# A decoder trunk on one core: two input projections of eight weight tiles turned from full products into seven products of quarters, with the sums of x made behind the memory weights

## The reference, cut to what matters

```python
proj = x @ w_in
cb, cc, ch, rq, rk, rv, rg, mq, gl = jnp.split(proj, split_idx, axis=-1)
conv_y, new_buf = short_conv(cc * ch, conv_buf, conv_w)
a_out = (cb * conv_y) @ w_conv_out
...                                            # retention branch: b_out
m_out = mem_attention(mq.reshape(b, t, MEM_HEADS, MEM_HEAD_DIM), mk, mv).reshape(b, t, MEM_WIDTH) @ w_mem_out
merged = g[:, :, 0] * a_out + g[:, :, 1] * b_out + g[:, :, 2] * m_out
x = layer_norm(DEEPNORM_ALPHA * x + merged @ w_out, ln1_g, ln1_b)
hdn = jnp.square(jax.nn.relu(x @ w_up))
x = layer_norm(DEEPNORM_ALPHA * x + hdn @ w_down, ln2_g, ln2_b)
```

## Time and profile before

| | |
|---|---|
| median of 3 runs | 2172.88 us (2172.08 to 2173.35) |
| the profiled execution, its own time | 2170.49 us |
| its span, first to last instruction | 2168.7 us |
| granted TensorE clock, mean | 0.993 |
| PE / PEld busy | 2127.2 us (98%) / 2081.6 us (96%), 16116 matmuls |
| POOL busy | 1326.5 us (61%) |
| DVE busy | 1081.6 us (50%) |
| ACT busy | 508.8 us (23%) |
| DMA | 215.23 MB, mean 99 GB/s |

### The profile page before, as it was taken

One profiled execution on the slowest core, in us unless ns is written; L12 is line 12 of the kernel. 1 busy time (PEld: TensorE's weight loads), 2 busy tenths in 40 slices (PEclk: granted clock), 3 DMA queues, 4 the chain that ended last, 5 costly groups with the idle time before them and its releaser, 6 DMA issues.

```text
span 2168.7 us, 39024 instructions
## 1 busy us (share of the span) xinstructions
PE 2127.2 (98%) x16116; PEld 2081.6 (96%) x16116; DVE 1081.6 (50%) x1713; ACT 508.8 (23%) x909; POOL 1326.5 (61%) x1545
## 2 busy tenths in 40 slices
PE   8999999999999999999999999999999999999997
PEld 8998999999998999999999989999999989999997
DVE  7156300543278873525791572006424787726257
ACT  3121111041013141414141210200410131514133
POOL 6644557645683948375866446676457759475574
PEclk9999999999999999999999999999999999999998
DMA  5314424234231323222324243342352313222321
GB/s 184 113 59 157 128 86 136 69 107 160 94 98 59 98 78 98 79 79 80 96 61 126 59 156 117 103 130 68 108 176 78 98 41 104 79 90 79 98 89 53
DMA packets 199928, 215.23 MB, mean 99 GB/s; under 512 B 5216, under 2 KB 192608, under 8 KB 199776
## 3 DMA queue, kind: packets, MB, share of 16 engines
q1 hardware_dynamic: 170304, 172.84, 25.6%
q10 hardware_dynamic: 29472, 40.20, 5.5%
HBM read 199.06 MB, written 13.97 MB: 98 GB/s over the span
## 4 chain that ended last, share of the span: by engine, by line
PE 94%; DVE 6%; issue 0%; ACT 0%; DMA 0%; ACTq 0%; DVEq 0%
PE gp L524 52%; PE gp L1038 12%; PE gp L540 7%; PE gp L550 7%; PE qb L630 6%; PE gp L693 4%; PE gp L867 1%; PE gp L879 1%; PE qb L661 1%; PE gp L688 1%; DVE r L2055 1%; DVE r L1946 1%; DVE dacc L1902 0%; DVE qb L1943 0%; DVE sqacc L1931 0%; DVE x_lo L1955 0%
## 5 line engine op out<-in xcount | busy, mean ns | idle before, releaser
L439 POOL TENSOR_TENSOR w_lo<-stage,w_hi 128x256 fp32r<-128x256 f32 x1072 | 869.2, 842 | 52.5 <-ACT w_hi L1250 30.0
L436 POOL TENSOR_SCALAR w_hi<-stage 128x1024 fp32r<-128x1024 f32 (+1 forms) x268 | 288.0, 1075 | 567.7 <-PE gp L524 256.9
L524 PE MATMUL gp<-x_hi,w_hi 128*128 128x288 f32 x1408 | 303.8, 297 | 0.0
L524 PE MATMUL gp<-b_hi,w_hi 128*128 128x288 f32 x1408 | 303.6, 297 | 0.0
L524 PE MATMUL gp<-x_lo,w_hi 128*128 128x288 f32 x1408 | 301.0, 295 | 0.0
L524 PE MATMUL gp<-x_hi,w_lo 128*128 128x288 f32 x1408 | 300.9, 295 | 0.0
L524 PE MATMUL gp<-b_lo,w_hi 128*128 128x288 f32 x1408 | 300.5, 295 | 0.0
L524 PE MATMUL gp<-b_hi,w_lo 128*128 128x288 f32 x1408 | 300.5, 295 | 0.0
L524 PEld LDWEIGHTS gp<-b_hi,w_hi 128*128 128x128 f32 x1408 | 226.5, 188 | 3.4 <-issue 3.1
L524 PEld LDWEIGHTS gp<-x_hi,w_hi 128*128 128x128 f32 x1408 | 226.8, 189 | 2.9 <-issue 2.6
L524 PEld LDWEIGHTS gp<-x_lo,w_hi 128*128 128x128 f32 x1408 | 226.6, 189 | 0.0
(11 more groups left out here) (275 smaller groups left out, 4368.0 us busy)
## 6 DMA issues: line engine op xcount, KB each, us to landing
stage<-in_w_in SPq DMA_DIRECT2D x62, 1024.0 KB, 5.8
stage<-in_w_up SPq DMA_DIRECT2D x32, 1024.0 KB, 5.4
stage<-in_w_down SPq DMA_DIRECT2D x32, 1024.0 KB, 5.0
stage<-in_w_ret_out SPq DMA_DIRECT2D x8, 1024.0 KB, 5.3
stage<-in_w_mem_kv SPq DMA_DIRECT2D x8, 1024.0 KB, 5.0
stage<-in_w_out SPq DMA_DIRECT2D x8, 1024.0 KB, 5.0
s_in_c<-in_ret_state ACTq DMA_DIRECT2D x8, 512.0 KB, 4.6
out_ret_sample<-s_in_c ACTq DMA_DIRECT2D x8, 512.0 KB, 3.4
```

The lines of the kernel that those rows point to most:

```text
L436: nc.gpsimd.tensor_scalar(hi, raw, 1.0, 1.0, ALU.mult, ALU.mult).then_inc(hi_done, 1)
L439: ins = nc.gpsimd.tensor_tensor(lo[:, k:k + 2, :], raw[:, k:k + 2, :], hi[:, k:k + 2, :].bitcast(F32), ALU.subtract)
L524: last = mm(gp[:, 2 * (i % 2) + half, 0:HALF], w[:, i % 4, k * P:(k + 1) * P], x(k, half), start=(n == 0), stop=(n == 3 * nk - 1))
```

## The change

`T_MQ` and `T_CC` are done as group 0 of seven products: four pairs, the first two giving `mq`, the last two `cc`. The sums of x for them lie in `q_hi` and `q_lo` (where `b_hi` and `b_lo` are, free there) and are made by DVE and ACT during `T_KV`; their scratch is `tmp`. The helpers take g, pair numbers count 16 a layer and not 12, and the functions move up in the file unchanged but for that. ACT's evacuation loop (L1273) goes. POOL makes for these tiles only the lows of the raw quarters. PE's wait for the sums of x stands inside `seven_products`, ahead of its third product, for group 0 and for group 1; before it stood ahead of group 1. `T_CH` and `T_CB` stay full products.

```diff
+    q_hi = place("q_hi", [P, 4, 4, HALF], F32R, a_bhi)
+    q_lo = place("q_lo", [P, 4, 4, HALF], F32R, a_blo)
     def pair_no(l, g, p):
+        return (l * 4 + g) * 4 + p
+    def hidden_no(l, g, p):
         return (l * 3 + g - 1) * 4 + p
+    def first_tile(g):
+        return T_FF + 16 * g if g else T_MQ
+    def out_of_pair(g, p):
+        return (relu, relu_odd)[p % 2] if g else (mq, cc)[p // 2][:, 2 * (p % 2):2 * (p % 2) + 2, :]
...
 POOL
-            with pool.Fori(0, (T_AM - T_MQ) // RING) as it:
-                split_four(l, it * RING + T_MQ)
+            seven_splits(l, 0)
+            split_four(l, T_CH, behind=(0, pair_no(l, 0, 3)))
+            split_four(l, T_CB)
...
 PE
-            with pe.Fori(0, 4) as j:
+            for p in range(4):
+                seven_products(0, p)
+            with pe.Fori(2, 4) as j:
                 for i in range(4):
                     product(l, j * 4 + T_MQ + i, j * 2 + (T_MQ + i) // 2, i, *X)
+                if p == 0 and g < 2:
+                    pe.wait_ge(s_split, l * 8 + 4 * g + 4)
                 pe.wait_ge(t_split, 4 * q + 1)
                 one(2, c, rows_sum(0), True)
...
-                    if g == 1:
-                        pe.wait_ge(s_split, l * 4 + 4)
...
 ACT
                 weights_high(T_KV + 4 + i)
+                if i % 2:
+                    sums_high(0, i // 2)
+            act.wait_ge(b_ready, l * 9 + 9)
             for i in (0, 2):
                 tile_is_done(act, l, T_KV + 5 + i)
...
+                if i == 0:
+                    raw_to_bank(0, 0)
+                    seven_high(0, 0, 0)
+                    seven_high(0, 0, 1)
+                    sums_high(0, 2)
+                else:
+                    seven_high(0, 0, 4)
+                    seven_high(0, 0, 2)
+                    sums_high(0, 3)
+                    seven_high(0, 0, 3)
+                    seven_high(0, 0, 5)
+                    seven_high(0, 0, 6)
             act.dma_start(kT_new[bass.ds(l, 1), :, :, :].rearrange("l p h m -> (l p) h m"), km[:, :, :]).then_inc(km_out, 16)
             act.dma_start(v_new[bass.ds(l, 1), :, :].rearrange("l (m p) c -> p (l m) c", p=P), vm[:, :, :]).then_inc(km_out, 16)
-            for t0, buf, s in ((T_MQ, mq, mq_ready), (T_CC, cc, cc_in)):
...
+            seven_aside(0)
...
 DVE, behind its last multiplication of T_RO
+            def x_total(g, k):
+                x_sum = x_sums if g else tmp
+                if k:
+                    dve.wait_ge(s_made, l * 8 + 4 * g + k)
+                for i in range(2):
+                    ins = vec_.tensor_tensor(x_sum[:, i, :], x_hi[:, 4 * i + k, :].bitcast(F32),
+                                             x_lo[:, 4 * i + k, :].bitcast(F32), ALU.add)
+                link(ins)
...
+            for k in range(4):
+                x_total(0, k)
+                if k:
+                    row_sums_low(0, k - 1)
+                x_parts(0, k)
+                if k == 2:
+                    weight_sum(0, 0, 1)
+            sum_low(0, 0, 1)
+            weight_sum(0, 0, 2)
+            weight_sum(0, 0, 3)
+            row_sums_low(0, 3)
+            sum_low(0, 0, 2)
+            weight_sum(0, 0, 4)
+            sum_low(0, 0, 3)
+            sum_low(0, 0, 4)
+            seven_aside(0, queries_or_gates)
```

More of the change, by code:

```diff
@@ new lines, in seven_high, with keep_part @@
+            def seven_high(g, p, n):
+                q = pair_no(l, g, p)
+                seven_free(act, l, g, p, n)
+                k_half, i = SEVEN[n]
+                if k_half is not None:
+                    act_fn(seven_slot(w_hi, n), quarter(p, k_half, i), ACT.Copy).then_inc(raw_high, 1)
+                else:
+                    act.wait_ge(t_made, 4 * q + i)
+                    act_fn(seven_slot(w_hi, n), t_sum((0, 1, 2, 3)[i - 1]), ACT.Copy).then_inc(t_high, 1)
+            def keep_part(q, n, bank, i):
+                act.wait_ge(prod_done, 7 * q + n + 1)
+                if q:
+                    act.wait_ge(quarter_made, 4 * (q - 1) + 4)
+                act_fn(part[:, i, :], gp[:, bank, 0:HALF], ACT.Copy).then_inc(part_in, 1)
@@ new lines, in hidden_high, with seven_aside @@
+            def hidden_high(g, p, i):
+                act.wait_ge(act_made, 2 * hidden_no(l, g, p) + 2 - i)
+                act_fn(b_hi[:, 2 * p + i, :], relu_of(p)[:, i, :], ACT.Copy).then_inc(act_high, 1)
+            def seven_aside(g):
+                for p in range(4):
+                    q, a, more = pair_no(l, g, p), (0, 3)[p % 2], p < 3
+                    if more:
+                        raw_to_bank(g, p + 1)
+                    keep_part(q, 0, a, 0)
+                    if more:
+                        seven_high(g, p + 1, 0)
+                    if g and p:
+                        hidden_high(g, p - 1, 0)
+                    if more:
+                        seven_high(g, p + 1, 1)
+                    keep_part(q, 2, 1, 1)
+                    if more:
+                        seven_high(g, p + 1, 2)
+                    keep_part(q, 3, a, 2)
+                    if more:
+                        seven_high(g, p + 1, 3)
+                        seven_high(g, p + 1, 4)
+                    keep_part(q, 5, a, 3)
+                    if more:
+                        seven_high(g, p + 1, 5)
+                    if g:
+                        hidden_high(g, p, 1)
+                    if more:
+                        seven_high(g, p + 1, 6)
@@ new lines, in seven_aside @@
+            def seven_aside(g, done):
+                for p in range(4):
+                    more = p < 3
+                    if more:
+                        weight_sum(g, p + 1, 1)
+                    quarter_out(g, p, 0)
+                    if more:
+                        sum_low(g, p + 1, 1)
+                        weight_sum(g, p + 1, 2)
+                        weight_sum(g, p + 1, 3)
+                        sum_low(g, p + 1, 2)
+                        weight_sum(g, p + 1, 4)
+                    quarter_out(g, p, 1)
+                    quarter_out(g, p, 2)
+                    done(p, 1)
+                    if more:
+                        sum_low(g, p + 1, 3)
+                    quarter_out(g, p, 3)
+                    done(p, 0)
+                    if more:
+                        sum_low(g, p + 1, 4)
```

314 lines of the change are left out of this document (129 added, 185 removed).

## The result

Over 15 runs of each the changed kernel takes 2181.95 us and the kernel before 2175.56. One of the 15 runs of the changed kernel took 7332 us and is left out of the ratio, the other 14 lie between 2176.5 and 2184.7: ratio 1.0028, interval 1.0019 to 1.0037. The forecast was 2176.6, 0.17% above a kernel before of 2172.88. The changed kernel is 5.4 us above the forecast, and 2.7 us of that is the kernel before itself, whose median is 2.7 us higher here and whose executions lie between 2171.6 and 2178.8. The profiled execution has a span of 2177.1 us where 2172.5 was forecast, at a mean granted clock of 0.988 (before 0.993).

A forecast was written before the change was run, and what follows sets the result against it. PE was taken to bound the kernel nearly throughout. Per layer -6.4 (fewer matmuls) - 2.2 (moved wait) + 6.0 (sums of x) + 4.5 (first pair) = +1.9, +3.8 in all: median 2176.6 us, range 2165.5 to 2182.

The forecast's parts named there:

- the first pair: First pair of products in T_MQ: PE waits at its third and fourth products, costing 4.5 us a layer, bounds 3 and 5.5.
- The third product: First pair in T_MQ: PE waits 2.5 us for DVE's last low of the sums of x.
- The fourth: First pair in T_MQ: the fourth product waits for ACT to copy the first one away, 2.0 us.
- Sums of x in the memory stage: Memory stage: DVE's sums slow POOL's lows, so PE waits at both value pairs; 6.0 us a layer, at most 10.5.
- rival 2: Memory stage: POOL and DVE take strict turns, costing 10.5 us a layer in place of 6.0; 2185.6 us, chance 0.07.
- Fewer matmuls: T_MQ and T_CC: 336 matmuls in place of 384 save 6.4 us a layer, 12.8 in all.
- Rival 4: T_MQ and T_CC: seven products not bound by PE, so 6.4 us a layer isn't saved; up to 2189 us, chance 0.04.
- The moved wait: Start of group 1: two products done first cover PE's wait for sums of x; gain 2.2 us a layer, 4.4 in all.
- Rival 3: Start of group 1: the moved wait gives nothing, as another input or `keep_part` is late; 2181 us, chance 0.05.
- Costed at nothing: Pairs 1 to 3, loading the first pair's weights, the end of pair 3 and ACT's removed copies: no time lost or gained.
- The sum: All terms: +1.9 us a layer, +3.8 in two layers; 2174.3 us profiled, 2176.6 as median, 0.17% above before.
- Rival 1: Memory stage: POOL's lows stay in time, so the 6.0 us loss drops out; 2164.7 us, chance 0.29.

The follow-up runs named there:

- e3: The changed kernel with idle matmuls filling PE's waits: 18 and 10 ahead of the two value pairs, 18 ahead of the third product. Ratio to the kernel before 1.0004.
- e6: The changed kernel with the totals of x for k = 0 to 2 partly in PSUM, so the parts read one SBUF input. Ratio to the kernel before 0.9988.
- e4: The changed kernel with group 0's sums of x made earlier, in T_RO, three of four totals in PSUM, two high parts moved ahead on ACT. 2154.0 us, ratio 0.9898.
- e5: The kernel before with one edit: PE's wait for group 1's sums of x stands ahead of its third product, not ahead of the group. Ratio 0.9965.
- e1: The kernel before with only the sums of x added in the memory stage on DVE and ACT, not used by anything. Ratio 1.0052.
- e2: The changed kernel without group 0's sums of x; products take quarters of x instead, so outputs differ. Ratio to the kernel before 0.9938.
- e7: The kernel before with three more POOL instructions ahead of the sixth memory tile's lows, no DVE work added. Memory stage through T_CC 82.35 / 82.33 us by layer, one execution.
- e8: The kernel before with five more POOL instructions ahead of the sixth memory tile's lows, no DVE work added. Memory stage through T_CC 85.19 / 83.69 us by layer, one execution.

## Why the prediction was right in direction and short in size

**The step that fell short is the price of a wait: the forecast put it at the length of the wait and put the granted clock behind it at nothing, without a reason.** The waits themselves it had right. Each is taken below from the starts of PE's matmuls. PE's timeline after, in layer 0, at the two waits of the first pair:

```profile
348.62 0.40 PE L917 MATMUL gp<-q_hi,w_hi 128*128 128x288 f32 x1 [2.52 <-DVE q_lo L1822]
...
352.24 0.58 PE L917 MATMUL gp<-q_hi,w_hi 128*128 128x288 f32 x1 [1.47 <-ACT part L1289]
...
354.05 0.44 PE L917 MATMUL gp<-q_lo,w_hi 128*128 128x288 f32 x1
354.29 0.44 PE L917 MATMUL gp<-q_hi,w_lo 128*128 128x288 f32 x1
...
357.16 0.29 PE L917 MATMUL gp<-q_hi,w_hi 128*128 128x288 f32 x1
357.29 0.30 PE L917 MATMUL gp<-q_lo,w_hi 128*128 128x288 f32 x1
```

At 354 the starts are 0.24 us apart, at 357 they are 0.13: TensorE's clock was at 1.2 GHz and then at 2.4 again. PE had been idle 2.5 us before 348.6 and 1.5 before 352.2.

*Each wait by its own step.* The third product was forecast 5.65 us behind the end of the value pairs, and it came at 348.62 - 342.78 = 5.84. The fourth was forecast at 9.3 to 9.8, and it came at 352.24 - 342.78 = 9.46. So the hand count of DVE's and ACT's orders held. The fourth product comes at 9.44 to 9.46 us in both layers, in e3 and in e6 too, whether the third one ran at the full pace (e3) or nearly all of it at half (layer 1): ACT's copy into `part` decides it. A fall of the clock between the two waits therefore costs nothing; it only makes the second wait shorter (1.47 us in layer 0, 0.64 in layer 1, 1.76 in e3). What costs is the slow stretch behind the last wait: 17 matmuls in layer 0 and 13 in layer 1 at 0.24 in place of 0.133 us, with the changes of pace at both ends 2.0 and 1.6 us. In sum: T_MQ with T_CC takes 51.46 us in e4, where nothing waits, and 56.38 in e3, where the waits stand and the clock holds. That is 4.9 us for the waits, where 4.5 was forecast. After it takes 58.44 and 57.97, 2.1 and 1.6 us more, and this is the clock.

The first of the two DMA issues ran beside ACT's copy of 349.99 to 350.59, at 350.00. The second, 350.44 to 351.06, ended 0.11 us ahead of `raw_to_bank`; the trace puts the 0.58 us of idling before that down to a low of DVE, and I can't tell the two apart. Together they cost ACT 0.6 us at most and not the 0.8 of the sum.

**Sums of x in the memory stage**: 6.0 us forecast, 5.7 and 7.1 measured. PE's waits at the two value pairs in layer 0:

```profile
328.18 0.38 PE L897 MATMUL gp<-w_hi,mt_hi 128*128 128x256 f32 x1 [2.41 <-POOL w_lo L453]
...
330.72 0.41 PE L897 MATMUL gp<-w_lo,mt_hi 128*128 128x256 f32 x1
330.93 0.41 PE L897 MATMUL gp<-w_hi,mt_lo 128*128 128x256 f32 x1
...
333.14 0.28 PE L897 MATMUL gp<-w_lo,mt_hi 128*128 128x256 f32 x1
...
336.93 0.39 PE L897 MATMUL gp<-w_hi,mt_hi 128*128 128x256 f32 x1 [1.24 <-POOL w_lo L453]
```

The step was right. The lows were forecast to be ready at 329.2 and 338.2 and came at 328.1 and 336.9, in a stage that began 0.8 us sooner; those from the fifth on, forecast at 17 to 18 us, took 17.6. The second value pair starts 22.84 us into the stage where it started at 17.28, so 5.6 us late where 6.0 was forecast. Behind the first wait the clock fell, and some 16 matmuls at 0.213 in place of 0.12 us took 1.5 us longer. They cost nothing: the second pair waits for POOL's lows in any case and starts at 22.90 us in e3, where the clock held, and only PE's second wait was shorter by them. In layer 1 it is the other way round:

```profile
1406.41 0.39 PE L897 MATMUL gp<-w_hi,mt_hi 128*128 128x256 f32 x1 [2.42 <-POOL w_lo L453]
...
1415.19 0.58 PE L897 MATMUL gp<-w_hi,mt_hi 128*128 128x256 f32 x1 [2.77 <-POOL w_lo L453]
...
1416.01 0.41 PE L897 MATMUL gp<-w_hi,mt_hi 128*128 128x256 f32 x1
1416.22 0.41 PE L897 MATMUL gp<-w_lo,mt_hi 128*128 128x256 f32 x1
```

All 48 matmuls behind the first wait start 0.12 us apart, so PE came sooner to the second pair, waited 2.77 us there, and then went at 0.21 us from the start. Here no wait follows that could take it up, and the memory stage is 30.12 - 28.69 = 1.4 us longer than in layer 0. One wait of 2.41 and one of 2.42 us, the same place and program, with and without a fall.

POOL kept 14.21 / 21.45 = 0.66 of its speed (forecast 0.7 and something for the lows). Strict turns, rival 2, would have put 10.5 us here.

The Trainium skill, "TensorE: Matmul & The Clock Gate", section "HAM oscillation — how this bites in real kernels", says that behind a long enough idle gap of PE the next work starts at the lower clock, and counts this beside the wait itself. The rows agree for most of the gaps of 2.4 to 2.8 us in this kernel, at 1.4 to 2.1 us where no other wait stands behind; they don't settle when a gap does it.

**Fewer matmuls**: 6.4 us forecast, 6.7 measured (58.18 - 51.46, in e4, where nothing waits; the 336 matmuls start 132.4 ns apart there and not 133.3). Rival 4 is out.

**The moved wait**: forecast 4.4 us "at most", the entry is gone in every kernel that has the change (e5 alone too), and 4.5 us goes at the place itself. "At most" was wrong: where the wait brings a fall of the clock, it is worth 1.5 us more a layer. That 4.4 us is gone outside the stages is luck. In the stretch from the 576 matmuls to the end of group 1 the profiled spans differ by 2.9 us, since these matmuls went at 133.3 ns in layer 1 after and at 130.0 before; the other 1.5 us lies in stretches that the change doesn't touch. Rival 3 is out.

**Costed at nothing**: right. No wait stands in pairs 1 to 3 of either layer, nor at T_CH.

**The sum.** Forecast +1.9 a layer and measured +4.2 (8.4 / 2). By terms, layer 0 and layer 1: fewer matmuls -6.7 for -6.4; sums in the memory stage +5.7 for +6.0; the first pair +4.9 for +4.5; the clock +2.0 and +3.0, for which the forecast had no term; outside the stages -2.2 as forecast, in part by luck. The clock's 5.0 us is all of the difference of 4.6 and a little more. That 2181.95 us lies inside the stated 2165.5 to 2182 is luck, by 0.05 us. It is outside the forecast's own range of 2172 to 2181; without the 2.7 us by which the kernel before rose it would be inside both. The two medians are 6.4 us apart where 3.8 was forecast. Whether the direction hung on the clock is not shown: by the spans the changed kernel would still be 8.4 - 5.0 = 3.4 us slower without its fall, but the median of e3 is only 1.0 us above the kernel before and its interval includes no change. Rival 1 was the mechanism that could have turned the sign. e4 shows that the loss it would save is real, and more: with POOL's slack kept, and DVE's and ACT's orders of the first pair cleared as well, the same products are 17.2 us faster in the span than before.

**Cause shown.** e1 adds the sums alone and gets the wait and the loss; e2 takes them away and the wait goes; e6 keeps their work and relieves only the operands, and 4.7 and 3.9 us a layer come back, of the 12.6 and 13.6 by which the stages stand above e4; e3 keeps all delays and restores only the clock, and 2 to 3 us a layer come back; e4 keeps all work and moves it, with three of four totals in PSUM, and everything comes back. What decides whether the clock falls behind a gap stays open. The wait of 2.12 us ahead of group 1 in the kernel before is followed by matmuls at the full pace in both layers, and the same wait in e1, e7 and e8 by a fall in four of six cases; 2.21 us in e8 and 2.41 us after are followed by a fall in layer 0 and not in layer 1; the two of 2.42 us in e1 both were; the seven waits of 2.5 to 3.1 us in these stages all were too. A wait of 0.8 to 1.8 us with PE at the full pace ahead of it was never followed by one there. The length of the gap alone doesn't tell.

The Trainium skill, "SBUF — State Buffer", section "SBUF: two separate sides", cited ahead of the result for the port pair that the two engines share, names as contending an operation of VectorE with two SBUF inputs. e6 agrees with this choice of instructions (0.45 us for a part with one input in PSUM, 0.88 with both in SBUF). That the other engine is blocked in full meanwhile is not what POOL's 0.66 shows.

## What to carry to other kernels

Work put behind a full engine is free only if each of the engines that it shares something with has slack at that place: look at the slack of the engine beside it (POOL here, 1.0 us against a loss of 7), and put the work in the stage where that engine waits for PE and not PE for it. Price a wait of PE as long as those here (2.1 us and more) by its length and by the matmuls at half the clock behind it, which was 1.4 to 2.1 us where it came. Count that only behind the last wait of a chain: a slow stretch ahead of another wait is taken up by that wait. Where two waits stand close behind each other, count both chains to their own ends, for taking away the first only uncovers the second.

## What the runs showed of the hardware that was not expected

- Behind a wait of PE of 2.1 to 3.1 us the granted clock can fall to its lower level, sometimes at once (1415.19 in layer 1) and sometimes after ten matmuls at the full pace (behind 328.18 in layer 0), and the same wait in the other layer may go without.
- A fall that is followed by another wait cost nothing (the second value pair at 22.84 us with the fall and 22.90 without; the fourth product at 9.46 us with and without).
- The same 576 matmuls ahead of group 1 started 130.0 ns apart in some cases and 133.3 ns in others, at a granted clock of 1.00 in both.
- Matmuls that compute nothing of use, put into the waits, made the kernel 0.24% faster than without them (1.0004 against 1.0028).
- An addition of 288 columns on DVE with both inputs in SBUF takes 0.88 us beside POOL's lows; with one input in PSUM 0.45, and POOL's 20 lows go from 21.45 to 18.79 us when 12 of 16 of these additions are changed so (their totals are then written to PSUM).
- A DMA issue on ACT's queue (0.41 us) ran wholly beside the ACT instruction ahead of it.
